# Moving the embedding's projection from the last stage into the end of the attention

## What is computed

```python
def second_block(x, p, w_in, w_o, ...):
    ...
        mix = jnp.concatenate([merge_heads(sb_out), merge_heads(diff_out)], axis=-1)
        h = h + mix @ w_o[i]

        xn = rmsnorm_2(h, g_ffn[i])
        u = causal_depthwise_conv_2(xn @ w_up[i], conv_w[i], conv_b[i])
        gate, val = jnp.split(u, 2, axis=-1)
        h = h + (jax.nn.gelu(gate) * val) @ w_down[i]

        xn = rmsnorm_2(h, g_ple[i])
        h = h + jax.nn.sigmoid(xn @ w_ple_gate[i]) * (p[i] @ w_ple_proj[i])
    return rmsnorm_2(h, g_final)
```

## Time and profile before

| | |
|---|---|
| median of 3 runs | 1909.64 us (1908.81 to 1911.33) |
| the profiled execution | 1910.33 us |
| span in its profile | 1908.6 us |
| PE busy | 1885.5 us, 99% of the span |
| DVE, ACT, POOL busy | 53%, 42%, 12% |
| mean granted PE clock | 0.996 of full |

### The profile page before, as it was taken

One profiled execution on the slowest core, in us unless ns is written; L12 is line 12 of the kernel. 1 busy time (PEld: TensorE's weight loads), 2 busy tenths in 40 slices (PEclk: granted clock), 3 DMA queues, 4 the chain that ended last, 5 costly groups with the idle time before them and its releaser, 6 DMA issues.

```text
span 1908.6 us, 21266 instructions
## 1 busy us (share of the span) xinstructions
PE 1885.5 (99%) x8693; PEld 1558.5 (82%) x8693; DVE 1020.5 (53%) x1279; ACT 794.9 (42%) x1061; POOL 227.8 (12%) x258
## 2 busy tenths in 40 slices
PE   9999999999999999999999999999999999999997
PEld 7888888878888788888888888888878888888885
DVE  5444443357455666664444444655565777774335
ACT  5423222246444656442232222556554444443234
POOL 2000001201300111130000022100004100000212
PEclk9999999999999999999999999999999999999998
DMA  4432323342242222423223223333213323223331
GB/s 160 165 101 88 101 98 99 100 158 92 74 144 66 89 89 89 143 89 100 98 91 109 91 97 100 122 100 100 89 34 111 100 89 110 89 97 104 97 111 55
DMA packets 54178, 192.66 MB, mean 101 GB/s; under 512 B 7016, under 2 KB 7272, under 8 KB 53184
## 3 DMA queue, kind: packets, MB, share of 16 engines
q1 hardware_dynamic: 48896, 169.89, 27.1%
q0 software_dynamic: 4176, 19.82, 3.1%
q10 hardware_dynamic: 1008, 1.58, 0.2%
HBM read 179.18 MB, written 11.03 MB: 100 GB/s over the span
## 4 chain that ended last, share of the span: by engine, by line
PE 93%; DVE 3%; ACT 2%; issue 1%; DMA 0%; DVEq 0%; SPq 0%; ACTq 0%
PE psum L1773 93%; ACT at L840 1%; DVE wl L1179 1%; DVE zv L1176 0%; DMA x<-in_xT 0%; ACT wh L840 0%; PE psum L2176 0%; DVE x L1173 0%; DVE at L1534 0%; DVE vl L1179 0%; DVE mg L1173 0%; DVE sl L1179 0%; ACT L836 0%; DVE us L1173 0%; ACT us L840 0%
## 5 line engine op out<-in xcount | busy, mean ns | idle before, releaser
L1773 PE MATMUL psum<-xh,wh 128*128 128x512 f32 x1760 | 694.3, 395 | 1.7 <-DVE wl L1179 1.3
L1773 PE MATMUL psum<-xh,wl 128*128 128x512 f32 x1760 | 685.3, 389 | 0.0
L1773 PE MATMUL psum<-xl,wh 128*128 128x512 f32 x1760 | 685.2, 389 | 0.0
L1179 DVE TENSOR_TENSOR wl<-wraw,wh 128x1024 fp32r<-128x1024 f32 (+1 forms) x314 | 401.5, 1286 | 397.3 <-ACT wh L840 396.2
L840 ACT ACTIVATE wh<-wraw 128x1024 fp32r<-128x1024 f32 (+1 forms) x314 | 325.5, 1047 | 361.1 <-PE psum L1773 359.5
L1773 PEld LDWEIGHTS psum<-xh,wh 128*128 128x128 f32 x1760 | 330.6, 188 | 78.6 <-issue 8.7
L1773 PEld LDWEIGHTS psum<-xl,wh 128*128 128x128 f32 x1760 | 330.7, 188 | 69.9 <-issue 2.9
L1773 PEld LDWEIGHTS psum<-xh,wl 128*128 128x128 f32 x1760 | 330.4, 188 | 69.2
L1632 POOL TENSOR_TENSOR ssq<-x 128x512 f32<-128x512 f32 x5 | 5.2, 1038 | 714.4 <-DVE x L1258 454.1
L1773 PE MATMUL psum<-wh,xh 128*128 128x512 f32 (+1 forms) x256 | 88.3, 345 | 0.4 <-ACT zv L840 0.4
L1773 PE MATMUL psum<-wh,xl 128*128 128x512 f32 (+1 forms) x256 | 86.0, 336 | 0.0
(11 more groups left out here) (313 smaller groups left out, 2210.4 us busy)
## 6 DMA issues: line engine op xcount, KB each, us to landing
wraw<-in_w_ffn SPq DMA_DIRECT2D x86, 512.0 KB, 3.3
wraw<-in_w_down SPq DMA_DIRECT2D x44, 512.0 KB, 3.2
wraw<-in_w_up SPq DMA_DIRECT2D x44, 512.0 KB, 3.5
wraw<-in_w_qg SPq DMA_DIRECT2D x28, 512.0 KB, 3.3
wraw<-in_w_att SPq DMA_DIRECT2D x24, 512.0 KB, 3.2
wraw<-in_w_dn SPq DMA_DIRECT2D x22, 512.0 KB, 3.3
wraw<-in_w_zu SPq DMA_DIRECT2D x16, 512.0 KB, 3.2
wraw<-in_w_zv SPq DMA_DIRECT2D x8, 512.0 KB, 3.5
```

Of the source, the lines that this page charges most:

```text
L1179: return e.tensor_tensor(dst, src, hi.bitcast(F32), ALU.subtract)
L1773: return e.matmul(dst, lhsT, rhs, start=start, stop=stop, skip_group_check=skip)
```

## The change

The eight tiles of the projection are made inside the last heads of the attention. Steps: Z0 loads the two halves of pT into the row buffers ssq and ssg, Z1 and Z2 split them into the attention's query buffer of head pair 5, Y0 to Y7 each make one tile (6 products into bank 6 or 7), copy it out of its bank (even ones by ACT, odd ones by DVE) into R1, ssq or ssg in turn, and POOL's queue stores that buffer in a DRAM tensor ppd (256 KB each). U and V are the splits of weight units 231 and 232, An.. the ao steps 0 to 3 of output pair 0, which came first before and now stand between later segments. Of the 41 unread products in this place 13 are left (5 and 8). The last stage has no psplit, pp and ppev any more; one load of 2 MB brings ppd back into pp_.

```diff
-    (226, 1): "D5.5", (226, 7): "S41.5 D5.6 S41.6", (227, 3): "S41.7", (227, 4): "D5.7 S41.8 D5.8",
+    (226, 1): "D5.5", (226, 3): "Z1", (226, 5): "Z2", (226, 7): "S41.5 D5.6 S41.6", (227, 3): "S41.7", (227, 4): "D5.7 S41.8 D5.8",
...
-    (0, 3): "D5.13 D7.3 D5.14 D7.4 D5.15 D7.5 D5.16 D7.6 D7.7 D5.17 S60.0 D7.8 D7.9 S60.1 D7.10 D7.11 S60.2 "
-            "S60.3 D7.12 D7.13 S60.4 D7.14 S60.5 S60.6 D7.15 S60.7 D7.16 S60.8 S60.9 D7.17 S61.0 S60.10",
+    (0, 3): "D5.13 D7.3 D5.14 D7.4 D5.15 D7.5 D5.16 D7.6 Y4 Y5 U D7.7 D5.17 S60.0 D7.8 D7.9 S60.1 D7.10 D7.11 Y6 S60.2 "
+            "S60.3 Y7 D7.12 V D7.13 S60.4 D7.14 A0.0 S60.5 S60.6 D7.15 S60.7 D7.16 S60.8 A0.1 S60.9 D7.17 S61.0 "
+            "S60.10 A0.2 A0.3",
...
+        elif c == "Y":
+            j = int(n)
+            for k in range(2):
+                yield ("pp", j, k, 228 + j // 4)
+            yield ("ppev", j)
...
     for n in range(4):
-        step("ao", 0, n, 228)
+        shorts(f"Y{n}")
         shorts(AO_AT.get((0, n), ""))
-    split(231)
+    split(233)
...
-    step("ple")
-    pair("pg", 0, 302)
-    for k in range(2):
-        step("psplit", k)
-    for j in range(8):
-        if j % 4 == 0:
-            split(304 + j // 4 + 2)
-        for k in range(2):
-            step("pp", j, k, 304 + j // 4)
-        if j < 3:
-            step("rs", "gple", j)
-        step("ppev", j)
+    step("ple", 1)
+    pair("pg", 0, 304)
+    for i in range(3):
+        step("rs", "gple", i)
     for j in range(2):
         step("pgev", j)
...
+    PP_BUFS = (R1, ssq, ssg)
...
+    ph, plo, pT = aq[:, slot_of[5], 0:2, :], aq[:, slot_of[5], 2:4, :], (ssq, ssg)
...
+    def pp_free(e, j):
+        if j < 3:
+            e.wait_ge(*ps_d.at(1))
+        else:
+            e.wait_ge(s_ppo[j % 3], 16 * (j // 3))
...
+                e.wait_ge(s_pin, 16)
                 mul(s, s, pp_[:, j, :]).then_inc(pg_d.sem, 1)
...
+            elif kind == "ppev":
+                j, = a
+                e.wait_ge(*pp_out(j))
+                e.dma_start(ppd[:, j, :], PP_BUFS[j % 3][:, :]).then_inc(s_ppo[j % 3], 16)
             elif kind == "ple":
                 e.wait_ge(*xs_lo.at("gple", 7))
-                e.dma_start(pT[:, :, :], D["pT"]).then_inc(s_p, 16)
+                for i in range(3):
+                    e.wait_ge(s_ppo[i], (48, 48, 32)[i])
+                e.dma_start(pp_[:, :, :], ppd).then_inc(s_pin, 16)
...
-                if k == 0 and j >= 4:
-                    e.wait_ge(*pp_a.at(j - 4))
+                if k == 0 and j >= 2:
+                    e.wait_ge(*pp_out(j - 2))
```

More of the change, by code:

```diff
@@ L114, in short_steps @@
             yield ("S2", int(n))
+        elif c == "Y":
[3 more added lines that the diff above has]
+            yield ("ppev", j)
+        elif c == "A":
+            yield ("ao", int(n), int(seg), 230 + int(n))
+        elif w in ("U", "V"):
+            yield ("split", 231 if w == "U" else 232)
+        elif c == "Z":
+            yield ("psplit", int(n) - 1) if n != "0" else ("ple", 0)
         elif c == "B":
@@ L307, in make_plan @@
     for n in range(4):
-        step("ao", 0, n, 228)
+        shorts(f"Y{n}")
         shorts(AO_AT.get((0, n), ""))
-    split(231)
+    split(233)
     shorts(AO_AT["second"])
     for n in range(4):
-        step("ao", 1, n, 229)
+        step("ao", 1, n, 231)
         shorts(AO_AT.get((1, n), ""))
-    split(232)
+    split(234)
     for n in range(4, 8):
         for p in range(2):
-            step("ao", p, n, 230 + p)
+            step("ao", p, n, 232 + p)
         shorts(AO_AT.get((1, n), ""))
-    split(233)
+    split(235)
     for p in range(4):
@@ L736, in _build @@
     pp_p = sig("s_pp_p", pp=lambda j, k, u: [j] if k == 1 and j % 4 != 3 else [])
-    pp_a = sig("s_pp_a", ppev=lambda j: [j])
+    pp_a = sig("s_pp_a", ppev=lambda j: [j] if j % 2 == 0 else [])
+    pp_d = sig("s_pp_d", ppev=lambda j: [j] if j % 2 else [])
+    s_ppo = [sem(f"s_ppo{i}") for i in range(3)]
+    s_pin = sem("s_pin")
     pg_d = sig("s_pg_d", pgev=lambda j: [(j, "t"), (j, "m"), (j, "x")])
@@ L1140, in _ @@
                 k, = a
-                e.wait_ge(s_p, 16)
-                act(ph[:, k, :], pT[:, k, :], ACT.Copy).then_inc(ps_a.sem, 1)
-            elif kind == "ppev":
+                e.wait_ge(s_p, 32)
+                act(ph[:, k, :], pT[k][:, :], ACT.Copy).then_inc(ps_a.sem, 1)
+            elif kind == "ppev" and a[0] % 2 == 0:
                 j, = a
+                pp_free(e, j)
                 e.wait_ge(*pp_done(j))
-                act(pp_[:, j, :], bank(PP_BANKS[j]), ACT.Copy).then_inc(pp_a.sem, 1)
+                act(PP_BUFS[j % 3][:, :], bank(6), ACT.Copy).then_inc(pp_a.sem, 1)
             elif kind == "pgev":
@@ L1578, in _ @@
                 e.wait_ge(*ps_a.at(k))
-                low(plo[:, k, :], pT[:, k, :], ph[:, k, :]).then_inc(ps_d.sem, 1)
+                low(plo[:, k, :], pT[k][:, :], ph[:, k, :]).then_inc(ps_d.sem, 1)
+            elif kind == "ppev" and a[0] % 2:
+                j, = a
+                pp_free(e, j)
+                e.wait_ge(*pp_done(j))
+                e.tensor_copy(PP_BUFS[j % 3][:, :], bank(7)).then_inc(pp_d.sem, 1)
             elif kind == "pgev":
@@ L1751, in _ @@
                     e.dma_start(b8[:, c, m, :], src).then_inc(s_b8[c], 16)
+            elif kind == "ple" and a[0] == 0:
+                e.wait_ge(*D_p.at(5, "q12"))
+                for k in range(2):
+                    e.dma_start(pT[k][:, :], D["pT"][:, k, :]).then_inc(s_p, 16)
+            elif kind == "ppev":
+                j, = a
+                e.wait_ge(*pp_out(j))
+                e.dma_start(ppd[:, j, :], PP_BUFS[j % 3][:, :]).then_inc(s_ppo[j % 3], 16)
             elif kind == "ple":
                 e.wait_ge(*xs_lo.at("gple", 7))
-                e.dma_start(pT[:, :, :], D["pT"]).then_inc(s_p, 16)
+                for i in range(3):
+                    e.wait_ge(s_ppo[i], (48, 48, 32)[i])
+                e.dma_start(pp_[:, :, :], ppd).then_inc(s_pin, 16)
             elif kind == "pgev" and 1 <= a[0] < 7:
@@ L2171, in _ @@
                         for i in range(3, j - 1, -1):
-                            if n == 7 and j == 0 and i >= 2:
-                                unread(bank(1), 7)
+                            if n == 7 and (j, i) == (0, 2):
+                                unread(bank(1), 5)
                             if j == 0 and i >= 2:
@@ L2202, in _ @@
                     if p == 0:
-                        for c in range(2):
-                            e.wait_ge(*bank67_free(("qk", 6), c))
+                        e.wait_ge(*pp_out(6))
+                        e.wait_ge(*pp_out(7))
                     else:
@@ L2225, in _ @@
                     e.wait_ge(*ps_d.at(k))
-                t = mm3(bank(PP_BANKS[j]), tiles(wh, u)[:, i, :], tiles(wl, u)[:, i, :], ph[:, k, :], plo[:, k, :],
+                t = mm3(bank(6 + j % 2), tiles(wh, u)[:, i, :], tiles(wl, u)[:, i, :], ph[:, k, :], plo[:, k, :],
                         k == 0, k == 1)
```

38 lines of the change are left out of this document (16 added, 22 removed), and 2 rows, old and new, of the table ATT_AT.

## The result

| | before | after |
|---|---|---|
| median of 15 runs each, same chip | 1909.83 us (1908.16 to 1911.33) | 1913.44 us (1910.99 to 1914.62) |
| span of the profiled execution | 1908.6 us | 1912.1 us |
| mean granted PE clock | 0.996 | 0.994 |

The ratio after to before is 1.0017, with a 95% interval from 1.0010 to 1.0024. The changed kernel is 3.6 us slower, 0.19%: a small but certain loss, just short of the 0.2% from which the prediction calls a kernel slower. The forecast was 1912.1, its range 1903 to 1916.

The account below looks back on a forecast made before the run. PE, holding 93% of the chain that ended last, was taken as the bound. Last stage -10.9 + 2.9 + 1.7 = -6.3 us, attention +7.1 + 1.7 = +8.8, together +2.5: median 1912.1 us, range 1903 to 1916.

Parts of the forecast that it names:

- Last stage, products removed: Last stage: 48 projection products of 0.228 us each leave PE's chain, 10.9 us less.
- Last stage, the new wait: Last stage: PE waits 2.9 us before pair 2 for its unit's split, queued on ACT behind tiles 0 and 1's evictions.
- Last stage, clock: Last stage: one fall to half clock behind the new wait costs 1.7 us.
- The load of pp_ at nothing: Last stage: the 2 MB load lands by 1850 to 1852, ahead of its first reader at 1855.0, and costs nothing.
- The slower rival: Last stage: pp_ lands late, up to 1915.0 us; chance 0.18 together with more lateness in the chain.
- step 3: Attention: Y6 and Y7 fill PE's old 1.69 us wait before D7.12's column sums, which come at 1419.5.
- step 2: Attention: tile 3's copy on DVE ahead of D5.13 delays D5.13, D7.4 and everything behind them, 1.2 us late.
- step 4: Attention: PE waits 5.3 us before S60.5 for al, behind a chain over ACT, POOL and DVE.
- the rival with a shorter chain: Attention: the chain to S60.4 isn't that late, without that wait 1905.1 us; faster rival's chance 0.17.
- the rival in which the clock holds: Same waits, but the clock holds behind one or both: 1.7 to 3.4 us less, 1908.7 to 1910.4; chance 0.20.
- step 5: Attention, behind S60.5: A0.2 and A0.3 add 12 products, 2.7 us; the same point is reached 7.1 us late.
- Attention, clock: Attention: one fall to half clock behind the new wait costs 1.7 us, bounds 0 and 2.6.

Follow-up runs that it names:

- e7_last: Changed kernel with last-stage splits moved ahead of the evictions and the evictions of a pair of tiles interleaved: 1908.11 us, -1.5 against before.
- e8_noproj: Kernel before with the embedding's projection left out altogether, the added tiles zero: 1903.97 us, -5.6 against before.
- e2_split: Changed kernel with the last stage's splits of pair 2's units and the single tiles moved ahead of the evictions: 1911.90 us, +2.2 against before.
- e11_fillA: Changed kernel with 20 unread products filling the attention's wait ahead of S60.5, nothing in the last stage: 1911.28 us, +1.3 against before.
- e9_y3: Changed kernel with tile 3's copy moved behind D5.14 from ahead of D5.13: 1913.56 us, +3.6 against before.
- e3_lateV: Changed kernel with unit 232's split moved from ahead of D7.13 to behind D7.14: 1909.14 us, -0.5 against before.
- e4_masks: Changed kernel with tile 6's copy and store moved behind S60.3, so POOL makes the masks first: 1911.14 us, +1.5 against before.
- e5_both: Changed kernel with unit 232's split behind D7.14 and tile 6's copy and store behind S60.3: 1906.40 us, -3.2 against before.
- e6_all: Changed kernel with the edits of e5_both and e7_last together: 1901.38 us, -8.2 against before.
- e10_best: e6_all with tile 3's copy moved behind D5.14 as well: 1901.51 us, -8.5 against before.

## Why the prediction held, and where it was off

The likeliest case came true: the median is 1.3 us above the forecast, and the waits stand where it put them. By its steps:

- **Last stage, products removed (-10.9).** Right. e7_last, where nothing else holds PE, shows -11.2 us there.
- **Last stage, the new wait (+2.9).** Right, and shown. It was 2.88 us, ended by DVE's wl at pair 2. e8_noproj shows that it comes from the removal alone, e2_split and e7_last that it is the place of the split behind the evictions. What the prediction did not see is the next wait behind it: with the split moved, the last evictions bound the stage (4.69 us). That changed nothing in the forecast; it decides what a repair is worth.
- **Last stage, clock (+1.7).** The 96 products took 1.6 us longer than before. What parts -5.9 from -6.3 lies in the last norm, whose final column sums took 1.63 us and not 1.12; that seems to belong to this execution and not to the change (1.12 in e11_fillA, which has the same waits there).
- **The load of pp_ at nothing.** Right. It was issued at 1850.68 and took 8.9 us, so it landed at about 1860; its first reader on DVE started at 1864.53 and had waited for ACT, not for it. The slower rival named here fell.
- **Attention, step 1 (psplit at nothing) and step 3 (the old wait gone).** Right: the column sums came at 1419.34 for 1419.5.
- **Attention, step 2 (+1.2).** The size was right (1.11 us from the account), and so were its dates: D5.13 at 1403.97 for 1404.0, ACT's exponentials at 1407.87 for 1408.1, the transposes at 1411.29 for 1411.4. But the cause it named, tile 3's copy on DVE ahead of D5.13, is not the only one: a second path, tile 2's copy on ACT ahead of D7.2's exponentials, is nearly as late (in the changed kernel ACT then waited 0.52 us for D5.13). The prediction doesn't have that copy; that it made no difference to the sum is luck. With tile 3's copy out of D5.13's way that path and the copy's own 0.6 us ahead of D7.4 take its place (e9_y3). Neither was removed by itself, so how the 1.1 us divide between them stays open.
- **Attention, step 4 (wait of 5.3).** Right, 4.97 us. Its two links outside the head's own chain are shown one by one: unit 232's split 2.6 us (e3_lateV), tile 6's copy and store ahead of the masks 1.8 us (e4_masks), both 4.4 (e5_both), which is all that the stretch had grown (4.42). So the rival with a shorter chain fell, and nothing in the chain was later than forecast; the rival in which the clock holds fell too, since it dropped behind both waits.
- **Attention, step 5 (+2.7 for A0.2 and A0.3).** Right: with no fall, S60.5 to the last stage takes 417.66 us, without the projection and without a fall 414.94, which is 2.7 less.
- **Attention, clock (+1.7).** This term was mis-sized. By e11_fillA the fall costs 2.4 us, within the bounds of 0 and 2.6 that were given. The prediction took one fall as always the same length, 3.4 us; behind the 4.97 us wait it lasted 6.8 us, 5.9 of them outside the wait. The old fall, subtracted at 1.3 us inside step 5, was 1.2 (416.13 less 414.94).

Sum as measured: attention +1.1 + 4.4 + 2.7 + 2.4 - 1.2 = +9.4, last stage -5.9, together +3.5 for the forecast's +2.5. The 1 us is 0.7 of clock in the attention and 0.4 in the last norm. The other 0.3 us of the 1.3 come from the step to the median: the forecast took it at 0.7 us below the profiled execution, as in the first three runs of the kernel before, and for the changed kernel it was 0.4 (1913.44 for 1912.1 + 1.7). One range in the prediction doesn't follow from its own terms: with 0 and 2.6 us of clock behind each wait the forecast runs from 1908.7 to 1913.9, not from 1910 to 1915. The measured 1913.44 lies in both.

The rule of the Trainium skill that the prediction weighed ("TensorE: Matmul & The Clock Gate", section "Why this matters for your kernels": no idle gaps of TensorE above about 3 us between bursts) would have let the clock hold at 2.88 us. Here it fell behind that wait in each of the seven profiles that hold it, and in e3_lateV's profile already behind 2.37 us. The traces don't agree with the figure; as a warning against gaps it stands.

## What to carry to other kernels

Products moved into the holes of another stage are cheap only in the engine that does them. What they cost here was the small work around them: one copy, one store and one split, set ahead of the steps for which PE waits, each queued in order on ACT, POOL or DVE. Move the helpers behind the chain's own steps, and look, in the stage that loses the work, for what was just in time before: both ends together turned +3.6 us into -8.2 here. Price a wait of TensorE at its length and the clock behind it, and expect that filling it gives back only the second.

## What was not expected of the hardware

- **How long the half clock lasts varies, whether it comes too.** Read in windows of 0.2 us, each of the 13 stretches at 0.50 that begin and end between D7's column sums and PE's last product, in all profiles together, lasted 3.4 us (seven of them) or 6.8 (six), none anything between. Behind the same wait of 2.88 or 2.89 us at pair 2 it was 3.4 us in five profiles (the changed kernel, e3_lateV, e4_masks, e9_y3, e11_fillA) and 6.8 in two (e5_both, e8_noproj), some 0.8 of them inside the wait. The longer one cost 1.2 us more: e5_both's last stage took 65.80 us, e11_fillA's 64.62, with the same waits. Behind all four waits of 4.97 us it was 6.8. Behind a wait of 1.68 us at D7's column sums e8_noproj's profile shows no fall at all, behind 1.69 us at the same place show one.
- **A wait of 2.4 to 2.7 us went either way.** Windows of e3_lateV behind 2.37 us of waiting, and of e4_masks behind 2.45 us:

```profile
1424.00:1425.00 1.00, 1.00 (x11) 0.97 0.00 0
1425.00:1426.00 1.00, 1.00 (x4) 0.50 0.00 0
1426.00:1427.00 1.00, 1.00 (x6) 0.50 0.57 74
```

```profile
1425.00:1426.00 1.00, 1.00 (x12) 1.00 0.40 160
1426.00:1427.00 1.00, 1.00 (x8) 1.00 0.00 0
```

  e4_masks' median lies 2 us above its profiled execution, and the clock over each whole execution says why: three of its 11 took 1909.19 to 1909.50 us at a mean clock of 0.996, eight 1911.05 to 1912.14 at 0.995. Most of them, then, seem to have had a fall that the profiled one lacks. Behind 2.70 us of waiting the last column sums ran at full clock in e6_all and e7_last (1.12 and 1.13 us) and at half in e10_best (2.05). What decides it in one execution is open.
- **The same goes for the long waits.** Of the changed kernel's 15 executions 13 took 1912.70 us or more at a mean clock of 0.994 or 0.995, two 1910.99 and 1911.25 at 0.996 and 0.997. So in one and the same program about 2.4 us go with the clock, the size that e11_fillA gives for the fall in the attention; which fall those two lacked no profile shows.
